# A streaming encoder step: forget sums spread by one f32r product, first pairs cut at a tile's edge, loads and row work in another order

## The reference

```python
def macaron_half(x, g_pre, g_post, w_in, w_out):
    return x + FFN_RES_SCALE * rms_norm(swiglu(rms_norm(x, g_pre), w_in, w_out), g_post)
...
def fox_block(q, k, v, cq, ck, qpos, kpos):
    s = jnp.einsum('bqhd,bkhd->bhqk', q, k).astype(jnp.float32) * (HEAD_DIM ** -0.5)
    bias = jnp.swapaxes(cq, 1, 2)[..., :, None] - jnp.swapaxes(ck, 1, 2)[..., None, :]
    mask = kpos[None, :] <= qpos[:, None]
    p = jax.nn.softmax(jnp.where(mask, s + bias, -jnp.inf), axis=-1)
    return jnp.einsum('bhqk,bkhd->bqhd', p.astype(v.dtype), v)
...
    for layer in range(DEPTH):
        xp = macaron_half(xp, ng[0], ng[1], ffn_w_in[layer, 0], ffn_w_out[layer, 0])
...
        xp = xp + rms_norm(mp, ng[3])
        xp = macaron_half(xp, ng[4], ng[5], ffn_w_in[layer, 1], ffn_w_out[layer, 1])
```

## Time and profile before

| | us |
|---|---|
| median of 3 runs | 2748.79 (2746.49 to 2749.85) |
| profiled execution, its own time | 2742.54 |
| its span | 2740.8 |
| PE busy | 2635.4 (96%) |
| VectorE, ScalarE, GpSimd busy | 1027.3, 886.6, 94.9 |
| products of the pairs (3 groups of 2976) | 2034.5 |

### The profile page before, as it was taken

One profiled execution on the slowest core, in us unless ns is written; L12 is line 12 of the kernel. 1 busy time (PEld: TensorE's weight loads), 2 busy tenths in 40 slices (PEclk: granted clock), 3 DMA queues, 4 the chain that ended last, 5 costly groups with the idle time before them and its releaser, 6 DMA issues. The chain is left out here.

```text
span 2740.8 us, 46255 instructions
## 1 busy us (share of the span) xinstructions
PE 2635.4 (96%) x19601; PEld 2409.8 (88%) x19601; DVE 1027.3 (37%) x1381; ACT 886.6 (32%) x1515; POOL 94.9 (3%) x86
## 2 busy tenths in 40 slices
PE   7999999999987988999999999999999989999998
PEld 7998997899756876999899799899979769989997
DVE  3232224433535665422223432222252464232234
ACT  4321223322434554432122343212243433321222
POOL 0000001000001221000000100000010010000001
PEclk9999999999998999999999999999999999999999
DMA  4222222223270002222222222222223112222222
GB/s 131 70 84 69 77 69 85 62 70 92 83 258 18 3 13 78 81 72 88 66 77 69 69 85 76 88 66 75 77 64 105 66 54 77 77 81 66 77 76 85
DMA packets 280404, 210.82 MB, mean 77 GB/s; under 512 B 24364, under 2 KB 236486, under 8 KB 280280
## 3 DMA queue, kind: packets, MB, share of 16 engines
q1 hardware_dynamic: 280280, 209.03, 25.3%
HBM read 201.94 MB, written 7.05 MB: 76 GB/s over the span
## 5 line engine op out<-in xcount | busy, mean ns | idle before, releaser
L458 PE MATMUL ps<-act_hi,pair_hi 128*128 128x320 f32 x2976 | 678.5, 309 | 0.0
L458 PE MATMUL ps<-act_lo,pair_hi 128*128 128x320 f32 x2976 | 678.2, 309 | 0.0
L458 PE MATMUL ps<-act_hi,pair_lo 128*128 128x320 f32 x2976 | 677.8, 309 | 0.0
L458 PEld LDWEIGHTS ps<-act_hi,pair_lo 128*128 128x128 f32 x2976 | 497.8, 188 | 0.0
L458 PEld LDWEIGHTS ps<-act_lo,pair_hi 128*128 128x128 f32 x2976 | 497.6, 188 | 0.0
L458 PEld LDWEIGHTS ps<-act_hi,pair_hi 128*128 128x128 f32 x2976 | 497.2, 188 | 0.3 <-issue 0.2
L420 DVE TENSOR_TENSOR pair_lo<-pair_raw,pair_hi 128x1024 fp32r<-128x1024 f32 x206 | 253.7, 1236 | 430.7 <-ACT pair_hi L416 430.7
L416 ACT ACTIVATE pair_hi<-pair_raw 128x1024 fp32r<-128x1024 f32 x206 | 215.8, 1052 | 466.1 <-PE ps L458 315.3
L494 PE MATMUL ps<-row_hi,hid_hi 128*128 128x512 f32 x880 | 346.8, 394 | 6.1 <-DVE row_lo L447 6.1
L494 PE MATMUL ps<-row_hi,hid_lo 128*128 128x512 f32 x880 | 345.1, 392 | 0.0
L494 PE MATMUL ps<-row_lo,hid_hi 128*128 128x512 f32 x880 | 344.9, 392 | 0.0
(11 more groups left out here) (381 smaller groups left out, 2549.6 us busy)
## 6 DMA issues: line engine op xcount, KB each, us to landing
pair_raw<-in_ffn_w_in_dram SPq DMA_DIRECT2D x176, 512.0 KB, 3.8
row_raw<-in_ffn_w_out_dram SPq DMA_DIRECT2D x176, 256.0 KB, 2.9
pair_raw<-in_even_w_in_dram SPq DMA_DIRECT2D x22, 512.0 KB, 3.8
norm_buf<-in_norm_g_dram SPq DMA_DIRECT2D x12, 512.0 KB, 4.6
y<-in_cache_fox_k_dram SPq DMA_DIRECT2D x4, 1024.0 KB, 7.5
y<-in_cache_fox_v_dram SPq DMA_DIRECT2D x4, 1024.0 KB, 6.7
norm_buf<-in_cache_fox_k_dram SPq DMA_DIRECT2D x4, 1024.0 KB, 8.1
norm_buf<-in_cache_fox_v_dram SPq DMA_DIRECT2D x4, 1024.0 KB, 5.4
```

What stands on the lines that cost most here:

```text
L458: mm = pe.matmul(ps[:, 2 * c + h, 0:HALF], w[c][:, k, :], a[:, k, h * HALF:(h + 1) * HALF], start=(k == 0 and w is pair_hi and a is act_hi ...
```

## The change

It has these parts.

1. The start: SyncE sends x tile 0, the gains, x tile 1, the first weight pair, then the other x tiles. In the first norm two tiles are finished ahead of the others, and the first half of the first pair takes these two tiles (256 columns), the second half three (384). Three transposes stand between the products (`FIRST_TURN_AT`).
2. First pairs of norms 1 to 5: the first half takes three whole tiles (384 columns), the second half two (256). The transposes of tiles 3 and 4 come after 15 and 33 products, formerly after 21 and 42. The outputs are read by two instructions each, for which the first pair's tile is taken out of the loops.
3. Streams: `f_twice` holds the cached log forgets twice side by side, so the sums come on 128 partitions; ScalarE writes them as f32r into act_hi, VectorE subtracts to leave the low part on partitions 64 to 127, and `sel_all` has ones for both. The keys and values of stream 1 are sent during the prompt attention.
4. gm_out: rows 2 to 5 and 9 to 12 are loaded into ws and ws_new, in another order of loads; seven head rows; the spatial products of tiles 3 and 4 stand between products and wait for `times_u`; each square of `act_norm_halves` stands after a row of its own.

```diff
-TURN_AT = ((0, 7), (1, 6))
+TURN_AT = {(0, 5): 3, (1, 3): 4}
+FIRST_TURN_AT = {(0, 4): 2, (0, 7): 3, (1, 3): 4}
...
-                f_raw = fb("f_raw", [P, KD, FOXH])
-                f_hi = fb("f_hi", [P, KD, FOXH], F32R)
-                f_lo = fb("f_lo", [P, KD, FOXH], F32R)
+                f_twice = fb("f_all_twice", [P, 4, 2 * NSEQ * FOXH])
+                f_raw = f_twice[:, 0, 64:128].rearrange("p (k h) -> p k h", k=KD)
+                sel_all = fb("sel_all", [P, NSEQ, P], F32R)
+                f_hi, f_lo = (sel_all[:, i, 0:KD * FOXH].rearrange("p (k h) -> p k h", k=KD) for i in range(2))
+                f_all = f_twice[:, :, 0:64]
+                logf_all = fb("logf_all", [P, 2 * NSEQ * FOXH])
...
-        c_all, out2 = xn_buf[0:NSEQ * FOXH, 2 * TOK:3 * TOK], xn_buf[:, 3 * TOK:3 * TOK + P]
+        c_all, out2 = act_hi[:, 4, :], xn_buf[:, 3 * TOK:3 * TOK + P]
...
+        def tiles_first(m):
+
+            return TT // 2 if m == 0 else TT - TT // 2
+
+        def two_banks(buf, b, m):
+
+            at = P * tiles_first(m)
+            return (buf[:, 0:at], ps[:, b, 0:at]), (buf[:, at:TOK], ps[:, b + 1, 0:TOK - at])
+
         def pe_first_pair(pe, n, m=None):
 
 
-            for c in range(2):
-                pe.wait_ge(s_pair_lo[c], n + 2)
-                pe.wait_ge(s_pair_read[c], n + 1)
             for h in range(2):
+                at = HALF if m is None else P * tiles_first(m)
+                cols = slice(at, TOK) if h else slice(0, at)
                 if m is not None:
-                    pe.wait_ge(s_alo, 5 * m + (5 if h else 3))
+                    pe.wait_ge(s_alo, 5 * m + (TT if h else tiles_first(m)))
                 for c in range(2):
+                    if h == 0:
+                        pe.wait_ge(s_pair_lo[c], n + 2)
+                        pe.wait_ge(s_pair_read[c], n + 1)
                     for k in range(KD):
-                        if m is not None and h == 0 and (c, k) in TURN_AT:
-                            pe_turn(pe, m, 3 + c)
+                        if m is not None and h == 0:
+                            t = (TURN_AT if m else FIRST_TURN_AT).get((c, k))
+                            if t is not None:
+                                pe_turn(pe, m, t)
                         for w, a in ((pair_hi, act_hi), (pair_hi, act_lo), (pair_lo, act_hi)):
-                            mm = pe.matmul(ps[:, 2 * c + h, 0:HALF], w[c][:, k, :],
-                                           a[:, k, h * HALF:(h + 1) * HALF],
+                            mm = pe.matmul(ps[:, 2 * c + h, 0:cols.stop - cols.start], w[c][:, k, :], a[:, k, cols],
...
+                    if m is None:
+                        act.activation(silu[:, :, :], wide(0), ACT.Silu).then_inc(s_pair_read[0], 1)
+                    else:
+                        for dst, src in two_banks(flat_silu, 0, m):
+                            ins = act.activation(dst, src, ACT.Silu)
+                        ins.then_inc(s_pair_read[0], 1)
...
-        def act_norm_halves(act, m, groups):
-            act.activation(warm[:, :], eps[:, 0:1], ACT.Sqrt)
+        def act_norm_halves(act, m, groups, tiles=range(TT)):
             first = 10 * (m - 1)
-            for t in range(TT):
+            for t in tiles:
+                if t == 0:
+                    act.activation(warm[:, :], eps[:, 0:1], ACT.Sqrt)
                 act.wait_ge(s_evict, (groups - 2) * TT + t + 2)
...
         def act_first_norm(act):
             act.wait_ge(s_const, 4)
             act.activation(warm[:, :], eps[:, 0:1], ACT.Sqrt)
-            for s in range(TT):
-                act_root_ahead(act, 0, s)
-                if s >= 2:
-                    act_turned(act, 0, s - 2)
-            split_ahead(act, act_split_pair, 0)
+            act_root_ahead(act, 0, 0)
+            act_root_ahead(act, 0, 1)
+            act_split_pair(act, 0, 0)
+            act_turned(act, 0, 0)
+            act_turned(act, 0, 1)
+            act_split_pair(act, 1, 0)
+            act_root_ahead(act, 0, 2)
+            act_root_ahead(act, 0, 3)
+            act_root_ahead(act, 0, 4)
+            act_turned(act, 0, 2)
             act_turned(act, 0, 3)
             act_turned(act, 0, 4)
...
                 if b == 1:
-                    sp.wait_ge(s_ol, PSTEPS)
+                    sp.wait_ge(s_bs, PSTEPS)
                 if b == 2:
                     sp_rwkv_loads(sp)
                 if b >= 2:
                     sp.wait_ge(s_tk, 2 * (b - 1))
                 sp.dma_start(k_cache[slot], io["cache_fox_k"][0, b].rearrange("(t p) h d -> p t (h d)", p=P))\
                   .then_inc(s_kc[slot], 16)
+                if b == 1:
+                    sp.wait_ge(s_bs, 2 * PSTEPS)
...
-                pe.wait_ge(s_fall, 16 * NSEQ)
-                rows = slice(0, NSEQ * FOXH)
                 for k in range(4):
-                    pe.matmul(ps[rows, 6, k * P:SEQ], f_all[:, k, :], tri_ones[:, 0:SEQ - k * P],
+                    pe.matmul(ps[:, 6, k * P:SEQ], f_twice[:, k, :], tri_ones[:, 0:SEQ - k * P],
                               start=(k == 0), stop=(k == 3))
                 for k in range(4):
-                    pe.matmul(ps[rows, 7, 0:P], f_all[:, k, :], tri_ones[:, P:2 * P], start=(k == 0), stop=False)
-                pe.matmul(ps[rows, 7, 0:P], logf_all[:, :], tri_streams, start=False, stop=True)\
+                    pe.matmul(ps[:, 7, 0:P], f_twice[:, k, :], tri_ones[:, P:2 * P], start=(k == 0), stop=False)
+                pe.matmul(ps[:, 7, 0:P], logf_all[:, :], tri_streams, start=False, stop=True)\
                   .then_inc(s_call, 1)
...
-            act.activation(c_all, flat[0:NSEQ * FOXH, 6 * 512:6 * 512 + TOK], ACT.Copy).then_inc(s_callr, 1)
+            act.activation(c_all, flat[:, 6 * 512:6 * 512 + TOK], ACT.Copy).then_inc(s_chi, 1)
...
+            dve.wait_ge(s_chi, 1)
+            dve.tensor_tensor(c_all[64:128, :], flat[64:128, 6 * 512:6 * 512 + TOK], c_all[64:128, :].bitcast(F32),
+                              ALU.subtract).then_inc(s_callr, 1)
...
         def pool_fox_setup(pool):
-            pool.wait_ge(s_xnew, 5)
-            pool.memset(sel_all[:, :, :], 0.0).then_inc(s_sel0, 1)
+            pool.wait_ge(s_logf, 1)
+            pool.memset(sel_all[:, :, :].bitcast(F32), 0.0).then_inc(s_sel0, 1)
             pool.wait_ge(s_sel0, 1)
             sel = sel_all[:, :, :].rearrange("p b (h q) -> p b h q", q=NEW)
             pool.affine_select(out=sel, in_=sel, compare_op=ALU.not_equal, fill=1.0, base=0,
                                pattern=[[-FOXH, NSEQ], [-1, FOXH], [0, NEW]], channel_multiplier=1).then_inc(s_sel, 1)
+            pool.wait_ge(s_sel, 1)
+            pool.affine_select(out=sel, in_=sel, compare_op=ALU.not_equal, fill=1.0, base=-NSEQ * FOXH,
+                               pattern=[[-FOXH, NSEQ], [-1, FOXH], [0, NEW]], channel_multiplier=1).then_inc(s_sel, 1)
+            pool.wait_ge(s_sel, 2)
...
-            pool.tensor_copy(logf_all[:, :].rearrange("p (b h) -> p b h", b=NSEQ),
-                             logf[:, 4:5, :].broadcast_to([P, NSEQ, FOXH]))
+            pool.tensor_copy(logf_all[:, :].rearrange("p (b h) -> p b h", b=2 * NSEQ),
+                             logf[:, 4:5, :].broadcast_to([P, 2 * NSEQ, FOXH]))
+            pool.wait_ge(s_fall, 16 * NSEQ)
+            pool.tensor_copy(f_twice[:, :, 64:128], f_all)
...
-                if i == KD + 3:
-                    act_norm_halves(act, m, before(stage, 2) + OUT_N)
+                if i >= KD + 3:
+                    act_norm_halves(act, m, before(stage, 2) + OUT_N, (i - KD - 3,))
...
-        early_rows[before("gm_out", 1)] = {i + 2: a for i, a in enumerate(gm_early)}
+        early_rows[before("gm_out", 1)] = {i + n: a for i, a in enumerate(gm_early) for n in (2, 9)}
...
+        def sp_gm_out(sp):
+            r1 = before("gm_out", 1)
+
+            def row(i):
+                sp_row(sp, i, r1, r1 // 2, gm_out_row(i))
+
+            row(0)
+            row(1)
+            row(6)
+            row(7)
+            sp_early_rows(sp, r1, range(9, 13), gm_out_row)
+            row(8)
+            row(13)
+            sp_new_v_and_first_pair(sp)
+            row(14)
+            row(15)
...
-                    pe.wait_ge(s_gated, t - 1)
+                    pe.wait_ge(s_gu, t - 1)
...
-            for t in range(TT):
+            def head(rows, t):
                 pe.wait_ge(s_glo, t + 1)
-                for k in range(HEAD_ROWS):
+                for k in rows:
                     if t == 0:
-                        if k == 0:
-                            pe.wait_ge(s_evict, g1 * TT + 1)
-                        if k == HEAD_ROWS - 1:
-                            spatial(3)
-                            spatial(4)
                         pe.wait_ge(s_row_lo, r1 + k + 3)
                     row_products(pe, KD, r1, act_hi, act_lo, 0, k, t)
+
+            pe.wait_ge(s_evict, g1 * TT + 1)
+            head(range(4), 0)
+            spatial(3)
```

(32 more changed lines are left out.)

88 lines of the change are left out of this document (58 added, 30 removed).

## The result

The changed kernel takes 2705.17 us (median of 4 runs, 2703.07 to 2712.54) and the kernel before, beside it, 2747.64 us (4 runs, 2743.51 to 2749.85): a ratio of 0.9852, 95% interval 0.9829 to 0.9875, so 42.5 us or 1.5% faster. The forecast was 2716.5 with 2709 to 2728. The profiled execution took 2703.47 us, its span 2701.3 us (before: 2742.54 and 2740.8).

The account below looks back on a forecast made before the run. TensorE was taken as the bound, busy 2635 of 2740.8 us, with about 105 us winnable. Gains 6.0 + 6.7 + 9.9 + 9.7 = 32.3 us from the median 2748.8 gave 2716.5, range 2709 to 2728.

Parts of the forecast that it names:

- The start: First norm and first weight pair: new load order lets products start at 15.5 us, not 22.06; gain 6.0 us.
- The first pairs: Norms 1 to 5: the 384/256 cut with earlier turns gains 1.35 us each, 6.7 us in all.
- 320's price: First pairs and start: a 256-column product costs 0.147 us like a 320-column one, not 0.12; 2724.3 us; chance 0.07.
- f32's rate: First pairs: narrow f32r products fall to f32 rate, 0.48 us for 256 columns; 104 us slower, 2820; chance 0.03.
- The streams: Eight streams: cheaper sel_all products and earlier loads of stream 1 gain 9.9 us, from 6.5 to 11.5.
- Key load 2: Streams: sent near 759 us, lands before PE wants it; keys(3) come at 775.9 for 783.3, 7.4 us won.
- the period: Streams: key loads sent two streams ahead set it, 7.7 us for 8.15; four periods win 1.6 us.
- The rival of early loads in vain: Streams: state loads take as long to issue and PE waits as now; streams give 2.5 of 9.9; 2723.9; chance 0.06.
- The gMLP and its output: Spatial products and output rows: shorter waits for gated tile 2 and the last rows gain 9.7 us, from 6.5 to 11.5.
- TensorE's order: gMLP output: tile 1 rows between the spatial products, waiting for times_u only, remove the gated tile 2 wait; 6.5 us won.
- the rival by which VectorE and GpSimd would add 2.8: gMLP output: POOL products and splits exclude each other, 2.8 us lost; with slower key load 2, 2722.7; joint chance 0.18.
- Nothing else moves: Outside the four places: waits in the three middle ffn stages (1.8 us) and the recurrent part stay.

Follow-up runs that it names:

- the second profile of before: The kernel before, unchanged, run and profiled once more as a check on the forecast's base; no time of its own is given.
- the added waits: Changed kernel with eight idle times of TensorE added in the ffn stages by POOL memset chains, run in two orders; no total time given.

## Why the prediction was right or wrong

**The base.** The changed kernel was 11.3 us faster than the forecast median of 2716.5, 3.8 us below the range. The larger half of the 11.3 is no step of the replay. I took the difference from the median of three runs, 2748.8, though the profiled run was 6.3 us lower and the sum was made against it. Over 55 runs the mean is 2742.5, the profiled time. From there the forecast is 2710.2, inside its range; what is left, 37.0 us won for 32.3, lies in the streams and the gMLP. Three runs whose clock differs say little about a median.

**The start** (6.0 forecast): 6.3 in the first pair of profiles, 6.8 against the second profile of before, 5.5 when undone. Right step by step.

**The first pairs** (6.7): 7.0 in the profiles, of which 0.6 at norm 1 are GpSimd's set-up and not the cut; 6.5 when undone. The price of 0.12 for 256 columns was right; both rivals on it (320's price, f32's rate) are out.

**The streams** (9.9): 11.8 and, against the second profile of before, 13.1. Key load 2 gave what it was given, 7.1 us for 7.4. The step that failed is the period: I had every key load land 8.5 us after it was sent and the period at (8.5 + TensorE's own work) / 2, so that only half of what the products save would count, and 7.7 us a period. In the profiles only two or three of the last five key loads are waited for by 1 us or more, and where none is, the period is TensorE's own 6.8; from keys(3) to keys(7) it is (797.20 - 767.09) / 4 = 7.5. With the f32 product it is (802.55 - 769.37) / 4 = 8.3: nearly all of the 0.87 us that the products save counts, and not half. The f32r products cost 0.34 and 0.06 us for my 0.23 and 0.2, the same sum:

```profile
751.42 0.51 PE L1334 MATMUL ps<-act_hi,sel_all 128*128 128x512 f32 x1
751.76 0.22 PE L1335 MATMUL ps<-act_hi,sel_all 128*128 128x128 f32 x1
751.82 0.43 PE L1337 MATMUL ps<-y,ident 128*128 128x128 f32 x2
```

The new wait for the low part was 1.66 us for 0.79, the 0.8 forecast. The rival of early loads in vain is out.

**The gMLP and its output** (9.7): 13.6 by the means, 7.5 of waits and 6.1 of clock. Two steps failed. The clock: I counted the low stretch behind the 3.73 us wait and none behind the others, though the old order also has waits of 2.5 and 3.0 to 4.1 us. And the cause: the 6.5 us were laid to TensorE's order, which is worth 2.2 when it alone is put back; the wait of 3.73 us hung as much on the place of row 4's split on ScalarE and VectorE. The new wait was 2.6 us in three pieces, not 3.6 for row 15, so the rival by which VectorE and GpSimd would add 2.8 is out.

**"Nothing else moves"** held for the waits outside the four places, but for the 0.37 us at norm 1. It didn't hold for the clock. That the total came out only 4.7 us off from the right base is no merit of the gMLP's step: its 9.7 was reached by a wrong cause and without the clock behind the other waits.

## What to carry to other kernels

On an engine that is 96% busy the price of a wait has two parts, its length and what the clock does behind it; of the added waits those of 3.2 to 5.7 us were followed, all but one, by a low clock that cost 1.9 to 2.9 us more, so long waits go first. A wait in front of the bound engine is often queued, not computed: look at what stands ahead of the late instruction in its own engine's order (a key load behind a value load, a gating behind a row's split) before moving anything on the engine that waits. Undo edits one at a time and all together; where two hide the same wait, neither alone shows its worth. Take the base of a forecast from many runs, and compare kernels at an equal granted clock.

## What was not expected of the hardware

The same kernel, with the same waits to 0.1 us at most places, took 137.4 to 142.1 us for the same 658 products of a stretch (clock 1.00 to 0.97), and the time of whole runs follows the granted clock by 1.5 to 2 us for each 0.001 (lines through 55 and 13 runs). Of two idle times of 3.23 and 3.24 us one was followed by a clock of 0.57 and the other by 1.00, and single waits of 1.8 to 2.0 us at the same place of the program were followed by it in some profiles and not in others (1.84 us at 2001.49 in the first profile of the changed kernel was; 1.80 us at 2005.59, the same place with the first pairs put back, wasn't). The clock also fell without any wait, in 13 of 19 profiles. A VectorE instruction of 1.29 us took 1.98 beside one of GpSimd, and that alone made TensorE wait.
